# Neighbourhood attention: the relative bias added to the scores by VectorE together with the maximum, instead of by identity products on TensorE

## The reference

```python
def row_block(args):                      # one row of the 4 x 64 grid of latent queries
    ...
    bias = jnp.where(in_win[None, None], bias, NEG_INF)
    s_lat = jnp.einsum('bqhd,bkhd->bhqk', q_row, k_band).astype(jnp.float32) * scale + bias
    s_ctx = jnp.einsum('bqhd,bkhd->bhqk', q_row, k_c).astype(jnp.float32) * scale
    p = jax.nn.softmax(jnp.concatenate([s_lat, s_ctx], axis=-1), axis=-1).astype(v.dtype)
    return (jnp.einsum('bhqk,bkhd->bqhd', p[..., :nl], v_band)
            + jnp.einsum('bhqk,bkhd->bqhd', p[..., nl:], v_c))
```

## Time and profile before

| | us |
|---|---|
| runs | 2112.8, 2112.16, 2109.52; median 2112.16 |
| the profiled execution | 2112.16 |
| its span, first to last instruction | 2110.4 |
| TensorE busy | 2085.8 (99%), granted clock 0.998 |
| VectorE busy | 1523.2 (72%) |
| ScalarE busy | 1065.3 (50%) |
| GpSimd busy | 156.1 (7%) |

### The profile page before, as it was taken

The page is one execution under the profiler, slowest core; times in us unless marked ns, Lnnn a source line. Parts: engine busy times, 40 slices in busy tenths (PEclk is TensorE's granted clock), DMA queues, the critical chain, the costliest instruction groups (busy, mean ns, idle before and its releaser), DMA issues.

```text
span 2110.4 us, 34559 instructions
## 1 busy us (share of the span) xinstructions
PE 2085.8 (99%) x14422; PEld 1896.8 (90%) x14422; DVE 1523.2 (72%) x2366; ACT 1065.3 (50%) x1615; POOL 156.1 (7%) x195
## 2 busy tenths in 40 slices
PE   9999999999999999999999999999999999999999
PEld 8999989999999998999997785898888888679997
DVE  6878897978887889898963577556545436767774
ACT  6443666443644366644463446345444334756663
POOL 1200202200220010220110000000000000100000
PEclk9999999999999999999999999999999999999999
DMA  7666535667566552677531111113222222104553
GB/s 283 240 230 220 213 100 223 245 237 264 198 230 239 204 213 100 246 279 255 197 141 59 61 61 67 55 51 136 100 100 95 87 98 80 61 20 166 187 181 127
DMA packets 47819, 334.88 MB, mean 159 GB/s; under 512 B 5612, under 2 KB 5692, under 8 KB 8368
## 3 DMA queue, kind: packets, MB, share of 16 engines
q1 hardware_dynamic: 37872, 267.47, 36.3%
q0 software_dynamic: 9792, 65.21, 8.1%
HBM read 331.61 MB, written 1.05 MB: 158 GB/s over the span
## 4 chain that ended last, share of the span: by engine, by line
PE 92%; DVE 4%; ACT 2%; issue 1%; DMA 0%; POOL 0%; DVEq 0%; ACTq 0%; POOLq 0%
PE PS L495 91%; PE PS L1283 1%; DVE WLO L2310 0%; DMA RAW<-in_even 0%; PE PS L1197 0%; DVE AC L2752 0%; DVE ACC L2549 0%; DVE PT L2593 0%; DVE STAT L2910 0%; DVE XB L2395 0%; ACT X L1640 0%; ACT WHI L1608 0%; ACT XHI L1638 0%; DVE XB L2703 0%; DVE WN L2597 0%
## 5 line engine op out<-in xcount | busy, mean ns | idle before, releaser
L2310 DVE TENSOR_TENSOR WLO<-RAW,WHI 128x2048 fp32r<-128x2048 f32 (+1 forms) x251 | 573.1, 2288 | 188.3 <-ACT WHI L1608 185.6
L495 PE MATMUL PS<-XB,WHI 128*128 128x256 f32 (+1 forms) x2704 | 624.6, 326 | 5.2 <-DVE XB L2395 1.3
L1608 ACT CAST WHI<-RAW 128x2048 fp32r<-128x2048 f32 (+1 forms) x246 | 465.1, 1894 | 283.8 <-DMA RAW<-in_dn_c 75.7
L495 PEld LDWEIGHTS PS<-XB,WHI 128*128 128x128 f32 x2704 | 455.1, 191 | 50.0 <-issue 6.0
L495 PE MATMUL PS<-XHI,WHI 128*128 128x272 f32 (+1 forms) x1760 | 498.4, 290 | 0.1
L495 PE MATMUL PS<-XHI,WLO 128*128 128x272 f32 (+1 forms) x1760 | 489.4, 287 | 0.0
L495 PE MATMUL PS<-XLO,WHI 128*128 128x272 f32 (+1 forms) x1760 | 481.2, 287 | 0.0
L495 PE MATMUL PS<-XB,WLO 128*128 128x256 f32 (+1 forms) x1352 | 436.6, 323 | 0.0
L495 PEld LDWEIGHTS PS<-XHI,WHI 128*128 128x128 f32 x1760 | 328.3, 188 | 1.7 <-issue 0.7
L495 PEld LDWEIGHTS PS<-XHI,WLO 128*128 128x128 f32 x1760 | 325.7, 188 | 0.2
L495 PEld LDWEIGHTS PS<-XLO,WHI 128*128 128x128 f32 x1760 | 322.2, 188 | 1.4 <-DVE XLO L2356 0.8
(11 more groups left out here) (402 smaller groups left out, 2622.7 us busy)
## 6 DMA issues: line engine op xcount, KB each, us to landing
AW<-in_ada POOLq DMA_DIRECT2D x48, 1024.0 KB, 7.2
RAW<-in_up_c SPq DMA_DIRECT2D x44, 1024.0 KB, 5.0
RAW<-in_up_a SPq DMA_DIRECT2D x42, 1024.0 KB, 5.1
RAW<-in_up_b SPq DMA_DIRECT2D x42, 1024.0 KB, 5.2
RAW<-in_mix SPq DMA_DIRECT2D x30, 1024.0 KB, 5.0
RAW<-in_dn_a SPq DMA_DIRECT2D x22, 1024.0 KB, 5.0
RAW<-in_dn_b SPq DMA_DIRECT2D x22, 1024.0 KB, 5.1
RAW<-in_dn_c SPq DMA_DIRECT2D x22, 1024.0 KB, 4.9
```

Of the source, the lines that this page charges most:

```text
L495: return pe.matmul(o, w, x, start=first, stop=last)
L1608: act.copy(WHI1[:, s, 0:w], RAW[:, s, 0:w]).then_inc(w1_high, 1)
L2310: v.tensor_tensor(WLO1[:, s, 0:w], RAW[:, s, 0:w], WHI1[:, s, 0:w].bitcast(F32), ALU.subtract)\
```

## The change

Both identity products and their wait are gone, and each pair's score products announce their own result. GpSimd multiplies the two loaded bias tiles in place by 8 (float32, 128 partitions x 2048 elements each) before it loads the three tables of the odd layer; it announces both on `pool2_step`, whose later values all move up by two. VectorE's `top` waits for that for pairs 8 to 15, takes the maximum over the 256 context columns only, and then runs a `tensor_tensor_reduce` that adds the bias to the 256 latent columns in place in the PSUM bank and takes the maximum of the result, starting from the first maximum (a pointer to one value per partition). The code is otherwise the same; `IDN8` is still loaded.

```diff
--- before.py
+++ after.py
@@ -300,7 +300,7 @@
 
 
         DQ_AT, KPE_AT, CKV_AT, ROTATED_AT = 2, 5, 7, 16
-        ROW_SET, BORDERS, HEADS_ZERO, KEY_ROPE = 1, (3, 5, 12), 6, 10
+        ROW_SET, BORDERS, BIAS_SCALED, HEADS_ZERO, KEY_ROPE = 1, (3, 7, 14), 5, 8, 12
         TAB_LOADED, NU_LOADED, MASK_LOADED, BIAS_LOADED, RT_LOADED = 16 * 9, 16 * 10, 16 * 11, 16 * 13, 16 * 16
         PARTS_OUT, GATES_OUT, CUM_OUT, NF_OUT = 1, 2, 3, 4
         PARTS_COPIED, GATES_ABS, LS_MIN, LS_DONE, CUM_COPIED, ROWS_COPIED, NF_COPIED = 1, 4, 5, 6, 7, 8, 9
@@ -675,6 +675,9 @@
             for n in range(2):
                 pool.dma_start(BIASES[n][:, :, :, :, :], A["bias"][:, 4 * n:4 * n + 4, :, :, :]).then_inc(tab_loaded, 16)
             pool.wait_ge(tab_loaded, BIAS_LOADED)
+            for n in range(2):
+                b = BIASES[n][:, :, :, :, :].rearrange("p a z r c -> p (a z r c)")
+                pool.tensor_scalar(b, b, float(NAD) ** 0.5, None, ALU.mult).then_inc(pool2_step, 1)
             for dst, name in ((RT[:, :, :], "rope2"), (PERM[:, :], "perm"), (QNG[:, :], "qkv_g")):
                 pool.dma_start(dst, A[name]).then_inc(tab_loaded, 16)
             pool.wait_ge(at_out, len(EVEN_PAIRS))
@@ -1264,13 +1267,7 @@
                         pe.wait_ge(at_exp, 2 * (base + p - at_once) + 2)
                     outs = [PS[:, banks[(2 * p + e) % len(banks)], :] for e in range(2)]
                     for e, (a, b) in enumerate(it["qk"]):
-                        last = mm(pe, outs[e][:, 0:it["keys"]], a, b, True, it["bias"] is None)
-                        if it["bias"] is None:
-                            last.then_inc(at_scores, 1)
-                    if it["bias"] is not None:
-                        pe.wait_ge(tab_loaded, BIAS_LOADED)
-                        for e in range(2):
-                            mm(pe, outs[e][:, CTX:L2], IDN8[:, :], it["bias"][e], False, True).then_inc(at_scores, 1)
+                        mm(pe, outs[e][:, 0:it["keys"]], a, b, True, True).then_inc(at_scores, 1)
 
                 def turn(p):
                     for e in range(2):
@@ -2907,7 +2904,15 @@
                     for e in range(2):
                         v.wait_ge(at_scores, 2 * (base + p) + e + 1)
                         src, m = PS[:, banks[(2 * p + e) % len(banks)], 0:w], STAT[:, c + e:c + e + 1]
-                        vs.link(v.tensor_reduce(m, src, AX.X, ALU.max))
+                        if pairs[p]["bias"] is None:
+                            vs.link(v.tensor_reduce(m, src, AX.X, ALU.max))
+                        else:
+                            v.wait_ge(pool2_step, BIAS_SCALED)
+                            vs.link(v.tensor_reduce(m, src[:, 0:CTX], AX.X, ALU.max))
+                            o = STAT[:, c + 2 + e:c + 3 + e]
+                            vs.link(v.tensor_tensor_reduce(src[:, CTX:w], src[:, CTX:w], pairs[p]["bias"][e], 1.0, m,
+                                                           ALU.add, ALU.max, o))
+                            m = o
                         v.tensor_scalar(STAT[:, c + 4 + e:c + 5 + e], m, -pairs[p]["scale"], None, ALU.mult)\
                             .then_inc(at_max, 1)
```

## The result

The changed kernel takes 2123.65 us in the median of 4 runs (2122.62 to 2124.13), the kernel before 2112.48 beside it (4 runs, 2109.52 to 2114.1). The ratio is 1.0053, with a 95% interval of 1.0037 to 1.0069: 0.5% slower, where 2109.8 and at most 2114.4 had been forecast. The profiled execution took 2124.13 us, of which 2122.3 is the span.

What follows compares the result with a forecast made beforehand. The prediction took TensorE to bound the attention stage up to pair 12 and VectorE from pair 13. From 2112.16 us, -5.53 + 0.11 + 0.96 = -4.46, plus 2.0 for held maps, gave about -2.4: 2109.8 us, range 2107.0 to 2114.4.

Steps and rivals of the forecast that it cites:

- T: Length of one GpSimd scaling of a bias tile, forecast at 1.89 us from its copy of 2048 elements.
- the hold: VectorE's two scaled maps of pair 3 wait for GpSimd's instructions in flight: +2.0 us, from 0 to 3.8.
- Rival 3: GpSimd's scaling is slow and the kernel ends slower: at T 5.1 the cost is 8.4, giving 2116.1 us; chance 0.10.
- One input, no second read: Argument against slow GpSimd scaling: a multiplication by a constant reads one input, as the 1.89 us copy does.
- Removed from TensorE: 16 identity products, 7.7 us in all; with TensorE still the bound, pair 12 would turn 6.75 us earlier.
- A head costs 1.04: VectorE's maximum (0.53) plus new instruction (0.51) per head of pairs 8 to 15, 0.24 us more than before.
- VectorE's order without gaps: VectorE's steps from 1289.10 to pair 12's first map summed to 21.70 us; pair 12 turns 5.53 earlier.
- The tail: From pair 12 on VectorE bounds: 0.11 us for its second map and 0.96 for the longer top(14) and top(15).
- Rival 2: TensorE's clock falls behind new idle time, costing at most 1.6 us, nothing where VectorE bounds: 2111.4; chance 0.16.
- Rival 1: GpSimd's instructions do not hold VectorE's maps: -4.46 us, so 2107.7, or 2106.9 at the lower end; chance 0.17.
- Rival 4: VectorE's new instruction pays twice in PSUM, 0.27 us more for each of 16 heads, 4.3 us: 2114.1; chance 0.07.
- Rival 5: The identity products weren't the bound and TensorE would idle in their place: 2112 to 2114 us; chance 0.05.

Runs made afterwards that it cites:

- pool_copy: Changed kernel with GpSimd copying the two bias tiles onto themselves instead of multiplying them by 8: 2113.86 us, ratio 1.0014.
- before_filled: Kernel before the change, with 2 and 1 products of ones on TensorE ahead of the turns of pairs 0 and 1: 2110.74 us, ratio 0.9996.
- filled: Changed kernel, queries scaled in ScalarE's copy, no GpSimd work, 3 and 5 products of ones on TensorE ahead of pairs 12 and 13: 2111.91 us, ratio 1.0001.
- low_later: Changed kernel, queries scaled by ScalarE, no GpSimd work, VectorE's waiting low part moved behind pair 14's maxima and pair 13's maps: 2109.21 us, ratio 0.9985.
- q_scaled: Changed kernel with the factor 1/8 put into ScalarE's existing copy of the queries and no work on GpSimd: 2112.86 us, ratio 1.0011.
- to_sbuf: Changed kernel without GpSimd's multiplications, the new instruction writing its sums to an SBUF scratch tile instead of PSUM: 2111.47 us, ratio 0.9996.
- no_scaling: Changed kernel without GpSimd's two multiplications, VectorE adding the bias as loaded: 2112.51 us, ratio 1.0010.

## Why the prediction was wrong

**The step that failed** is the length of GpSimd's scaling: T = 1.89 us, taken from its copy. A multiplication of 128x2048 takes 5.37. The rule by which T enters held. Each us counts twice because two maps are held one after the other, so the prediction's own formula gives 1278.46 + 2 x 5.37 - 1280.24 = 8.96 us; VectorE's second map ends 8.64 late on the stage's clock, and pair 4 turns 9.00 late. That the last two numbers agree so well with the formula is in part luck, as TensorE's first products behind the hold ran at the low clock. Rival 3 named the mechanism, its factor of two and the break-even at T = 3.1, and its upper T of 5.1, from the two-input row, was near the truth; its chance of 0.10 was too low.

**T was not all of it.** With T = 5.37 the prediction's sum is 2112.16 - 4.46 + 8.96 = 2116.7, still 7 us short. Two more terms were wrong: the gain without the hold was put at 4.46 and is 1.7, and the clock was set against the other rivals as an alternative, at a chance of 0.16, where it comes along with every wait that the change makes. The pool_copy run has the T that was assumed: its hold is near the forecast, but its stage is 5.0 us longer than without work on GpSimd, not 2.0, and its time is 2113.86, not 2109.8. So the forecast would have been too low with the right T as well. "One input, no second read" was the argument that made the copy the nearest row. The row of the same operation was not in the trace, and with ends at 1.89 and 5.1 on either side of a break-even at 3.1, the chance should have been shared out more evenly.

The page of the Trainium skill that was weighed against the row points the right way: by "GPSIMD Engine Reference", section 3.1, the estimate was 4.4 us, from its figure for two inputs, and the trace has 5.37 with one input, so it is nearer than the copy's 1.89. What became of the maps stands in the Trainium skill's "SBUF — State Buffer", section "Who interferes with whom", as a lock that the first instruction to issue holds for its whole length; the two maps that end 0.15 us behind a multiplication agree with that, the free maps beside the short pieces are not explained by it.

**Without the hold** the forecast was -4.46. At the full clock the runs show -1.7: before_filled's stage of 64.15 against filled's 62.42. Where the other 2.7 went, by the steps:

- *Removed from TensorE*: right. The products are gone, and TensorE waits for VectorE ahead of pairs 7, 9, 12 and 13.
- *A head costs 1.04*: it costs 1.11 to 1.12 (1304.10 to 1305.21 in VectorE's timeline), 0.06 of which is the accumulator read behind a result in PSUM. Twelve heads ahead of pair 12 make 0.9 us.
- *VectorE's order without gaps*: it has 0.36 and 0.30 us of waiting for scores and 0.28 of issue in these steps, 0.9 us that the layout did not have. With both, pair 12 turns 3.4 earlier and not 5.5 (45.43 in low_later, whose order is the same up to there and whose start ran at the low clock as well, against 48.84); 0.3 of the miss stays open.
- *The tail*: 1.07 lost by forecast, 1.6 measured at the full clock (3.33 ahead at pair 12, 1.73 at the output); four heads at 0.32 are 1.3 of it.

**Rival 2, the clock**, came true beside rival 3, and dearer than "nothing where VectorE is the bound" to 1.6: 2.2 us in the tail alone (64.63 against 62.42). The prediction had the idle time ahead of pair 13 right (2.2 forecast, 2.33 measured) and then let VectorE's bound hide the fall. The filled run shows that it does not: a turn of 1.97 for 1.1 us lies on the path between VectorE's maps and ScalarE's copies.

It came a second time, behind the hold. Up to pair 12 low_later is the changed kernel without work on GpSimd, with the same low start (turns in us from the first maximum):

```
pair                   4      7      9     12
low_later          15.56  24.83  32.32  45.43
after minus it     +9.01 +10.18 +10.17 +10.18
```

Between pairs 4 and 7, where the granted clock is 0.50 until about 1296, 1.2 us more are lost, and none behind that. From pair 12 to the output product the changed kernel takes 20.45 us and q_scaled 20.44, so the tail of the one is that of the other.

**The sum**: -1.7 for the change at the full clock, +9.0 for the hold up to pair 4, +1.2 for the stretch behind it, +2.2 for the clock of the tail make +10.7 of the measured 10.8. That the 1.2 is the clock's is read from the traces; no run filled that gap.

**Rival 1**, no hold, did not occur with the long instructions. **Rival 4** is refuted by to_sbuf. **Rival 5** too: at the same order and clock the identity products are worth 2.2 us.

## What to carry to other kernels

Before work is moved to GpSimd, look for a row of the same operation, not of the same size: here the copy takes 1.89 us and the multiplication 5.37, and what VectorE does beside it pays for it, once for each instruction that it is held at. A constant factor belongs where an engine copies the data anyway. And where a change makes TensorE wait in a chain of short steps, price the clock as well: what an engine wins ahead of a wait can be lost in the low stretch behind it, until the step that waits is put behind the work that does not. And add such costs up: two rivals that exclude each other in a forecast can come together on the chip.

## What the runs showed of the hardware that was not expected

- A multiplication by a constant on GpSimd, 128x2048 in float32, takes 5.37 us, 2.8 times its copy of the same shape (1.89 and 1.96). In pieces of 128x256 one takes 0.85.
- VectorE's scaled maps are held to the end of a long GpSimd instruction (0.35 becomes 3.67 and 5.34, and 1.70 and 1.79 beside the copies), but beside sixteen short ones of the same kind, which kept GpSimd over 90% busy, seven of eight maps lasted 0.35 and one 0.42. Why the short ones don't hold them stays open.
- VectorE's read of its accumulator takes 0.14 us when the elementwise result went into PSUM and 0.08 when it went into the SBUF.
- Idle times of 1.47 and 2.33 us with 4.4 us of work between them were followed by about 10 us of TensorE at 1.2 GHz, in the changed kernel, no_scaling and q_scaled alike. Products of ones in these gaps kept it at 2.4 GHz.
